# A decoder block on one core: the first norm's root on ScalarE, four orders of work, and the sums inside the last half tiles

## The reference

```python
mod  = silu(c) @ w_ada + b_ada                     # six vectors: shift1, scale1, gate1, shift2, scale2, gate2
h    = rms_norm(x, norm1_w) * (1 + scale1) + shift1
proj = h @ w_in                                    # 8 retention heads (q, k, v, gate), 8 differential heads (q, k, v)
y    = concat(retention(proj), diff_attention(proj))   # each head normed: group norm, or RMS norm
x    = x + gate1 * (y @ w_out)
h2   = rms_norm(x, norm2_w) * (1 + scale2) + shift2
x    = x + gate2 * (relu(h2 @ w_mlp1) ** 2 @ w_mlp2)   # inner width 8192
out  = rms_norm(x, final_norm_w)
```

## Time and profile before

| | us |
|---|---|
| runs, median of 3 (lowest, highest) | 2343.6 (2343.4, 2343.84) |
| the profiled execution, time | 2344.19 |
| its span, from first to last instruction | 2342.4 |
| mean granted clock of TensorE | 0.998 |
| busy: PE, DVE, ACT, POOL | 2320.1, 1256.4, 721.7, 90.7 |
| moved by DMA | 327.21 MB |

### The profile page before, as it was taken

How to read it: one execution, slowest core, us unless ns; L and a number is a source line. 1 busy time by engine, 2 the same in 40 slices (tenths; PEclk the granted TensorE clock), 3 DMA queues, 4 the chain that set the end, 5 groups by cost and what they waited for, 6 DMA issues and landing times.

```text
span 2342.4 us, 28296 instructions
## 1 busy us (share of the span) xinstructions
PE 2320.1 (99%) x10432; PEld 1891.1 (81%) x10432; DVE 1256.4 (54%) x1577; ACT 721.7 (31%) x1013; POOL 90.7 (4%) x59
## 2 busy tenths in 40 slices
PE   8999999999999999999999999999999999999998
PEld 5578888887888888888888888888888888888887
DVE  8989888866666675633333333333333333333354
ACT  3333333344445322421321321322222222222233
POOL 0011112101010000000000000000000000000000
PEclk9999999999999999999999999999999999999999
DMA  9965767622223573222222222222222222222222
GB/s 388 410 240 205 260 244 261 232 81 81 81 79 106 201 282 122 99 96 93 99 99 98 90 98 98 92 98 97 98 98 90 98 98 96 99 92 98 99 90 99
DMA packets 89575, 327.21 MB, mean 140 GB/s; under 512 B 8625, under 2 KB 9137, under 8 KB 89521
## 3 DMA queue, kind: packets, MB, share of 16 engines
q1 hardware_dynamic: 89232, 326.34, 38.8%
q10 hardware_dynamic: 290, 0.16, 0.0%
HBM read 322.27 MB, written 4.19 MB: 139 GB/s over the span
## 4 chain that ended last, share of the span: by engine, by line
PE 92%; DMA 3%; DVE 2%; issue 1%; ACT 0%; POOL 0%; ACTq 0%; POOLq 0%; DVEq 0%
PE bank L478 29%; PE bank L482 29%; PE bank L479 29%; DMA prob<-ada 3%; PE bank L689 1%; PE bank L655 1%; DVE w_lo L1209 1%; DVE ada_sb L1215 0%; PE bank L680 0%; PE bank L594 0%; PE bank L523 0%; PE bank L535 0%; PE bank L672 0%; PE bank L827 0%; PE bank L633 0%
## 5 line engine op out<-in xcount | busy, mean ns | idle before, releaser
L478 PE MATMUL bank<-act_hi,w_hi 128*128 128x512 f32 x2016 | 790.7, 392 | 0.3 <-ACT w_hi L885 0.3
L479 PE MATMUL bank<-act_lo,w_hi 128*128 128x512 f32 x2016 | 785.3, 390 | 0.0
L885 ACT ACTIVATE w_hi<-raw 128x1024 fp32r<-128x1024 f32 x393 | 415.0, 1056 | 835.4 <-PE bank L482 825.8
L1209 DVE TENSOR_TENSOR w_lo<-raw,w_hi 128x1024 fp32r<-128x1024 f32 x393 | 496.3, 1265 | 293.6 <-ACT w_hi L885 280.1
L482 PE MATMUL bank<-act_hi,w_lo 128*128 128x512 f32 x2016 | 498.2, 389 | 0.1
L478 PEld LDWEIGHTS bank<-act_hi,w_hi 128*128 128x128 f32 x2016 | 378.4, 188 | 81.2 <-ACT w_hi L885 2.3
L482 PEld LDWEIGHTS bank<-act_hi,w_lo 128*128 128x128 f32 x2016 | 378.3, 188 | 79.1 <-DVE w_lo L1209 0.5
L479 PEld LDWEIGHTS bank<-act_lo,w_hi 128*128 128x128 f32 x2016 | 378.7, 188 | 77.9
L478 PE MATMUL bank<-u_hi,w_hi 128*128 128x512 f32 (+1 forms) x1040 | 401.6, 387 | 0.0
L479 PE MATMUL bank<-u_lo,w_hi 128*128 128x512 f32 (+1 forms) x1040 | 400.2, 386 | 0.0
L1631 DVE SCALAR_TENSOR_TENSOR xy<-bank,modr,xy 128x512 f32 (+1 forms) x141 | 105.8, 750 | 412.3 <-PE bank L482 412.3
(11 more groups left out here) (176 smaller groups left out, 1304.7 us busy)
## 6 DMA issues: line engine op xcount, KB each, us to landing
raw<-weights SPq DMA_DIRECT2D x400, 512.0 KB, 3.3
ada_sb<-ada SPq DMA_DIRECT2D x78, 1024.0 KB, 5.1
xy<-x_t SPq DMA_DIRECT2D x16, 512.0 KB, 4.8
prob<-ada SPq DMA_DIRECT2D x8, 1024.0 KB, 10.4
ada<-ada SPq DMA_DIRECT2D x7, 1024.0 KB, 8.7
out<-rows_out SPq DMA_DIRECT2D x8, 512.0 KB, 4.1
ada_sb<-ada SPq DMA_DIRECT2D x4, 512.0 KB, 11.4
decay_sb<-decay SPq DMA_DIRECT2D x8, 256.0 KB, 3.3
```

The costliest lines, as they stand in the source:

```text
L478: pe.matmul(acc, stationary, hi, start=first, stop=False)
L479: pe.matmul(acc, stationary, lo, start=False, stop=False)
L885: nc.scalar.activation(w_hi[:, w], raw[:, r], ACT.Copy).then_inc(hi_ready, 1)
L1209: nc.vector.tensor_tensor(w_lo[:, w], raw[:, r], w_hi[:, w].bitcast(F32), ALU.subtract).then_inc(lo_ready, 1)
```

## The change

- *First root.* `token_mean(1)` and `token_root(1)` are gone. ScalarE loads the table of ln and exp after its last SiLU, computes exp(-0.5 ln(mean + eps)) from the bank of sums, and VectorE refines it in three 128x4 operations (`first_root`).
- *First stage.* Row 1 is loaded whole and dotted behind the root; the cast of the identity moves in between the sums of squares. For each even tile `act_lo` is now made ahead of `w_lo`, except for the last (14), whose `w_lo` goes ahead of the dot of row 30.
- *Four orders.* Head 0: `means_of_v` ahead of the modulation dot. The head before the first differential one: `var_eps` ahead of `rest_w`. Second norm: `normed_part(2, 0)` ahead of `rest_w`. First up group: `w_hi` of its ninth chunk (`C_MLP + 9`) after two of the four tiles instead of after all.
- *The end.* `last_sums(0)` and the transpose of tile 15's first half run inside `down_part(6, ...)`, before the seventh of the eight blocks of its first two passes. Half 0 is scaled as soon as its root is there, and the left half rows no longer wait for the last tile. In `last_sums` the wait for the last square stands behind the first four sums. The third row's left half is scaled and stored in two quarters, nine stores in all.
- GpSimd's roots count one mean less (`pool.wait_ge(tok_v_ready, n - 1)`).

```diff
@@ -134,7 +134,7 @@
 RESTS = (9, 11, 1, 3, 5, 7, 13)
-HALF_ROWS = (0, 1, 2 * KT - 1)
+HALF_ROWS = (0, 2 * KT - 1)
 SPLIT = tuple(k for k in range(KT) if k not in WHOLE)
@@ -181,8 +181,10 @@
     if not a.above(A_RET):
-            return a.base % NADA_1, a.base // NADA_1 + (1 if a.base % NADA_1 >= 2 else 0)
-    return a.place(NADA), a.value(NADA, -(-A_RET // NADA_1) - A_RET // NADA)
+        slot = a.base % NADA_1
+        return slot, a.base // NADA_1 + (1 if slot else 0)
+    slot = a.place(NADA)
+    return slot, a.value(NADA, A_RET // NADA_1 - A_RET // NADA + (1 if slot else 0))
@@ -232,6 +234,7 @@
         minus_half = sb("minus_half", [P128, TB])
+        ln_eps = sb("ln_eps", [P128, 1])
         mod1 = sb("mod1", [P128, KT, 2])
@@ -354,6 +357,7 @@
         newton, half_ready, turned = sem("newton"), sem("half_ready"), sem("turned")
+        first_ln, first_exp, first_newton = sem("first_ln"), sem("first_exp"), sem("first_newton")
         rotated_hi, rotated = sem("rotated_hi"), sem("rotated")
@@ -455,23 +459,33 @@
                     load_raw(Count(C_MLP + j, (4, i)))
-            for part in range(2):
-                for half in range(2):
-                    cols = slice(half * HALF, (half + 1) * HALF)
-                    for tb, scaled in ((2 * part, scaled_v), (2 * part + 1, scaled_s)):
-                        sp.wait_ge(scaled, 2 * part + half + 1)
-                        sp.dma_start(out[tb * P128:(tb + 1) * P128, cols], rows_out[:, tb, cols]).then_inc(out_written, 16)
-            sp.wait_ge(out_written, 32 * TB)
+            def store(tb, cols, scaled, count):
+                sp.wait_ge(scaled, count)
+                sp.dma_start(out[tb * P128:(tb + 1) * P128, cols], rows_out[:, tb, cols]).then_inc(out_written, 16)
+
+            left, right = slice(0, HALF), slice(HALF, D)
+            store(0, left, scaled_v, 1)
+            store(1, left, scaled_s, 1)
+            store(0, right, scaled_v, 2)
+            store(1, right, scaled_s, 2)
+            store(2, slice(0, HALF // 2), scaled_v, 3)
+            store(2, slice(HALF // 2, HALF), scaled_v, 4)
+            store(3, left, scaled_s, 3)
+            store(2, right, scaled_v, 5)
+            store(3, right, scaled_s, 4)
+            sp.wait_ge(out_written, 16 * 9)
...
         def _(pe):
-            def split_products(pairs, s, done=chunk_done):
+            def split_products(pairs, s, done=chunk_done, between=None, at=None):
...
                 for i, acc, hi, lo, first, _, ready in pairs:
+                    if at is not None and i == at:
+                        between()
                     if ready is not None:
@@ -828,11 +842,11 @@
-            def down_part(b, s, part, done):
+            def down_part(b, s, part, done, between=None, at=None):
...
                 split_products([(i, bank[b][:, cols], u_hi[:, i, cols], u_lo[:, i, cols], i == 0, i == BLOCKS - 1, None)
-                                for i in range(BLOCKS)], s, done)
+                                for i in range(BLOCKS)], s, done, between, at)
@@ -847,9 +861,10 @@
                 pe.wait_ge(ssq_ready, TAIL_SUMS + KT - 1 + part)
-                pe.wait_ge(sq_ready, TAIL_SQUARES + KT + 2 * part)
                 blocks = (2 * part, 2 * part + 1)
                 for n, source in enumerate((ssq, sq[:, 1])):
+                    if n == 1:
+                        pe.wait_ge(sq_ready, TAIL_SQUARES + KT + 2 * part)
                     for tb in blocks:
@@ -865,9 +880,11 @@
             turn_part(KT - 2, 0, KT - 1)
-            down_part(6, s0 + 30, 1, chunk_done)
-            last_sums(0)
-            turn_part(KT - 1, 0, KT)
+            def first_rows_end():
+                last_sums(0)
+                turn_part(KT - 1, 0, KT)
+
+            down_part(6, s0 + 30, 1, chunk_done, first_rows_end, 6)
             down_part(7, s0 + 31, 1, chunk_done)
@@ -985,7 +1002,7 @@
-                act.wait_ge(half_ready, 2)
+                act.wait_ge(half_ready, 3)
                 act.wait_ge(ve_ready, hp + 1)
@@ -1049,6 +1066,12 @@
                     nc.scalar.activation(silu_c[:, i * TOK:(i + 1) * TOK], bank[i][:], ACT.Silu).then_inc(silu_ready, 1)
+            load_table(LN_EXP_SET)
+            act.wait_ge(half_ready, 3)
+            act.wait_ge(mean_done, 1)
+            nc.scalar.activation(tok_r[:], ps_a[:, 0:TB], ACT.Ln, scale=LN_SCALE, bias=ln_eps[:, 0:1]).then_inc(first_ln, 1)
+            act.wait_ge(first_ln, 1)
+            nc.scalar.activation(tok_r[:], tok_r[:], ACT.Exp, scale=-0.5, bias=ln_shift[:, 0:1]).then_inc(first_exp, 1)
             act.wait_ge(vec_landed, 16)
@@ -1146,7 +1169,8 @@
                     for half in range(2):
-                        round_w(s0 + (2 * t + half + 1))
+                        if not (first and t == 0 and half == 0):
+                            round_w(s0 + (2 * t + half + 1))
                     take_u(g, 4 * q + t, t, s0 + (2 * t + 2), SPARE_UP if first and t == 0 else None)
@@ -1155,6 +1179,8 @@
             for t in range(4):
+                if t == 2:
+                    round_w(Count(C_MLP + 9))
                 take_u(0, t, t, Count(C_MLP + 8))
@@ -1179,7 +1205,8 @@
                 act.wait_ge(tok_r_ready, 4 + tb // 2)
-                act.wait_ge(tile_ready, KT + 2 * (tb // 2))
+                if half == 1:
+                    act.wait_ge(tile_ready, KT + 2 * (tb // 2))
                 row = rows_out[:, tb, half * HALF:(half + 1) * HALF]
@@ -1193,8 +1220,8 @@
             last_part(KT - 1, 0, 2)
+            scale_row(1, 0)
             last_part(KT - 2, 1, 3)
-            scale_row(1, 0)
             scale_row(1, 1)
@@ -1231,6 +1258,16 @@
                                                ALU.mult, ALU.add, to).then_inc(dot_done if half else half_dotted, 1)
+
+            def first_root():
+
+                dve.wait_ge(first_exp, 1)
+                nc.vector.scalar_tensor_tensor(tok_v[:], ps_a[:, 0:TB], NORM_EPS, tok_r[:], ALU.add, ALU.mult)\
+                    .then_inc(first_newton, 1)
+                dve.wait_ge(first_newton, 1)
+                nc.vector.scalar_tensor_tensor(tok_v[:], tok_v[:], -0.5, tok_r[:], ALU.mult, ALU.mult).then_inc(first_newton, 1)
+                dve.wait_ge(first_newton, 2)
+                nc.vector.scalar_tensor_tensor(tok_r[:], tok_v[:], 1.5, tok_r[:], ALU.add, ALU.mult).then_inc(tok_r_ready, 1)
@@ -1309,6 +1346,9 @@
                     nc.vector.tensor_tensor(ssq, ssq, square_at(m), ALU.add).then_inc(ssq_ready, 1)
+                    if m == 9:
+                        dve.wait_ge(ident_landed, 16)
+                        nc.vector.tensor_copy(ident_r[:], ident_early).then_inc(const_ready, 1)
@@ -1468,8 +1508,10 @@
                     at = j - 1 if head1 else j
-                    if at == 1:
+                    if at == 1 and not head1:
                         means_of_v(h - 1)
+                    if j == 5 and dif:
+                        var_eps(h - 1)
                     if not (head1 and j == 0):
@@ -1477,12 +1519,13 @@
                         rotate_q(h, s0 + 2, dif)
-                    if j == 5:
+                    if j == 5 and not dif:
                         var_eps(h - 1)
...
                         decay_strips(h - 1)
+                        means_of_v(h - 1)
                     for _ in range(slots[j]):
@@ -1522,25 +1565,25 @@
             first_square_sums()
-            dve.wait_ge(ident_landed, 16)
-            nc.vector.tensor_copy(ident_r[:], ident_early).then_inc(const_ready, 1)
             dve.wait_ge(vec_landed, 16)
...
             half_dot(0, 0)
-            token_mean(1)
             dve.wait_ge(silu_ready, 4)
             half_dot(0, 1)
-            half_dot(1, 0)
-            half_dot(1, 1)
+            first_root()
+            dot1(0, 1)
             normed(0, 0)
...
             for k in range(1, KT):
+                if k == KT - 1:
+                    rest_w(Count(k - 1))
                 dot1(k, 0)
...
                 if behind_split:
-                    rest_w(Count(k - 1))
                     modulated_rest(0, k - 1)
+                    if k < KT - 1:
+                        rest_w(Count(k - 1))
                     normed(0, k)
@@ -1665,9 +1708,9 @@
             modulated_rest_part(1, 0)
+            normed_part(2, 0)
             rest_w(Count(C_MLP))
             token_mean(3)
-            normed_part(2, 0)
             normed_part(3, 0)
@@ -1754,11 +1797,12 @@
-            def scale_row(tb, half):
+            def scale_row(tb, first, last):
                 dve.wait_ge(tok_r_ready, 4 + tb // 2)
-                dve.wait_ge(tile_ready, KT + 2 * (tb // 2))
-                row = rows_out[:, tb, half * HALF:(half + 1) * HALF]
+                if last > HALF:
+                    dve.wait_ge(tile_ready, KT + 2 * (tb // 2))
+                row = rows_out[:, tb, first:last]
                 nc.vector.tensor_scalar(row, row, tok_r[:, tb:tb + 1], None, ALU.mult).then_inc(scaled_v, 1)
@@ -1773,24 +1817,25 @@
```

(19 more changed lines are left out.)

## The result

The changed kernel takes 2359.1 us (median; 2358.7 to 2359.8) where the kernel before, on the same chip, takes 2343.7. The ratio is 1.0067 with the interval 1.0057 to 1.0077. The forecast was 2340.3 us, its range ended at 2342.0, and slower had been given a chance of 0.03.

The account below looks back on a forecast made before the run. PE was taken to bound most of the kernel, bytes the first stage, stores the end. Terms 0.59 + 0.32 + 0.66 + 0.42 + 0.5 + 0.8 = 3.3 us took the median 2343.6 to 2340.3 us; range 2338.7 to 2342.0.

Parts of the forecast that it names:

- the sum: Whole kernel: the gains at the stage end, four reordered waits and the output end add up to 3.3 us.
- start, inside the stage: First norm's root 0.8 us sooner and `act_lo` ahead of `w_lo`: both worth 0, covered by the stream of bytes.
- stage end: End of the first stage: chunk 14's `w_lo` ahead of row 30's dot brings later work 0.59 us sooner; bounds 0.3, 1.1.
- head 0, `means_of_v`: Head 0, before its values are used: `means_of_v` ahead of a 2.3 us dot readies `v_tok` sooner, about 0.32 us.
- `var_eps`: First differential head: `var_eps` ahead of a `w_lo` gets out of PE's way, 0.66 us.
- second norm: `normed_part(2, 0)` ahead of `w_lo` removes PE's wait for `act_hi`, 0.42 us; 0.1 comes off if `w_lo` is late.
- first up tiles: First up group: `w_hi` of chunk 9 rounded after two tiles instead of four removes PE's wait, about 0.5 us.
- tail: Output end: earlier sums and stores end the kernel 0.8 us sooner, with one break in the stream; bounds 0.4 and 1.4.
- The start counts too: Rival: the first root's 0.8 us reaches the end, giving 4.1 us, 2339.5; chance 0.17 together with all upper bounds.
- The first power is slow wherever it stands: Rival: GpSimd's 1.99 us first-run price moves to the second norm, about 0.5 us lost, 2340.8; chance 0.08.
- PE at the lower clock: Rival: shifted early PE work keeps the 1.2 GHz level longer, slower from 13 us on, near 2347; chance 0.03.
- Replaced by others: Rival: other waits 0.2 us later replace those removed, gain below 1.8 us, around 2342.5; chance 0.10.

## Why the prediction was wrong, point by point

**The failed step** is the sum, which has a term for every wait and none for PE's work. The prediction took the products' 0.23 us as given (24 of 0.23 us in a pair of chunks) and said of the gains that "PE runs without a wait behind each of them, so what is saved stays saved". It never counted the new tensor. `ln_eps` moved the moving operand of 3,024 products by 32 bytes against the weights: the kernel before with that displacement alone was 18.5 us slower. The diff names the allocation. No row of before could price its effect, since there every operand stands at distance 0, but the rows gave the scale: 92% of the chain is PE, and 1% of 0.2267 us on 3,024 products is 6.9 us, twice the whole sum.

**The rest held.** In the kernel with `ln_eps` out of the way, from the starts of the n-th product against the kernel before:

| term | forecast, us | measured, us |
|---|---|---|
| start, inside the stage | 0 | 0 (root back: no change; the new waits for `xy` too) |
| stage end | 0.59 | 0.59 (from the landing of row 30 to the start of product 400: 19.86 to 19.90, mean 19.88, in the thirteen kernels with the old order; 19.27 to 19.32, mean 19.29, in the five with the new one) |
| head 0, `means_of_v` | 0.32 | 0.40 (products 400 to 600) |
| `var_eps` | 0.66 | 0.59 (1800 to 2000) |
| second norm | 0.42 | 0.49 (4000 to 4200) |
| first up tiles | 0.50 | 0.62 (4200 to 4400) |
| tail | 0.8 | 0.83 (product 4400 to the end of the execution: 1360.23 before, 1359.40 here, 1360.22 with the old end put back); timed 0.88 |
| sum | 3.3 | 3.52; from the landing of row 30 to the end 3.50; timed 3.81 |

A wait's figure plus 0.16 us was the right price of a hand-over, within 0.12 us each time.

**The tail's hole.** In the kernel with `ln_eps` behind the heads' tensors, the first part's sums start at 2322.46, the stores at 2325.19, and the last rows' power ends at 2330.60 (compare):

```profile
2322.46 0.50 PE L869 MATMUL bank<-inv_d,ssq 128*128 128x1 f32 x4
...
2325.19 8.97 SPq L464 DMA_DIRECT2D out<-rows_out  x9
...
2329.91 0.69 POOL L1840 TENSOR_TENSOR tok_r<-tok_v,minus_half 128x2 f32<-128x2 f32 x1 [5.54 <-DVE tok_v L1798]
```

The stores start 4.7 us sooner than in the kernel before, where 3.9 had been written. The sums start 4.49 sooner, 3.05 of it from upstream (2.5 in the forecast; 0.4 is an earlier row 30) and 1.44 from their new place (1.43 in the forecast), and the power takes 0.69 us where it had taken 0.92.

The stream breaks once, as forecast, for 0.7 us where 0.5 had been worked out: the window there moved 254 GB/s in 2 us, against 399 in the one ahead (columns as in the earlier trace rows).

```profile
2328.00:2330.00 2.00, 1.44 (x12) 1.12 (x10) 0.97 (x3) 0.81 (x2) 0.09 (x1) 1.00 1.01 399
2330.00:2332.00 2.00, 0.00 (x0) 0.00 (x0) 1.26 (x4) 1.21 (x2) 0.60 (x1) 1.00 0.64 254
```

**The rivals.** *The start counts too*: refuted by the root put back. *The first power is slow wherever it stands*: refuted, the first power of the changed kernel is that of the second norm and takes 0.70 us (at 920.64), as the same one did before behind another (at 922.49), so the 1.99 went with its place or its four columns. *PE at the lower clock*: the one rival with the right sign, and not what happened: the granted clock stands at the full level from 26.56 to 2351.03 us of the changed kernel without a break (27.42 to 2334.83 before), and its first eight products with chunk 0 take 3.48 us and the next eight 2.01, as before. *Replaced by others*: true inside the first stage alone, where 2.9 us of waits for `xy` came in and cost nothing; behind it no wait took the place of those that went, and the table has the gains. The side "slower" had one mechanism only and so 0.03.

**The rest of the difference.** The displacement alone and the change without it sum to 18.5 - 3.8 = 14.7 us; 15.4 were measured. The traces say where the 0.7 lies. Row 30 lands at times between 114.52 and 115.89 us in the eighteen profiles, early and late with the old order and with the new. From its landing to the end of the profiled execution the kernel before takes 2228.64 us, the one with 32 bytes of `pad` 2247.69, the changed one 2243.97, and the changed one without the displacement 2225.14. So behind the landing the displacement costs 19.05, the change gains 3.50 without it and 3.72 with it, and the two add up to within 0.3 us. By these profiles what is left of the 0.7, and of the timed 3.81 against 3.50, lies ahead of the landing. Why a row lands a microsecond sooner in one execution than in another, no run tells.

**Left open.** What in the memory or in TensorE makes a distance cost, and why it reaches two products beyond the last displaced load.

## What to carry to other kernels

A new tensor is an edit to every tensor behind it. Where PE is the bound, compare the addresses before and after, keep each moving operand at the distance from the weights that the fast kernel has (here 0 modulo 512 bytes), and put new small tensors last or pad them to that multiple (in the run with `w_lo` moved by 32 bytes, 480 bytes behind it kept the other products at their old 227 ns). And when a change is small against the work that it leaves alone, the risk is in that work: one look at the mean duration of each unchanged group (here 390 against 395 ns) tells more than all the waits.

## What the runs showed of the hardware

TensorE's spacing at 512 columns and the full 2.4 GHz level depends on where the moving row and the weights stand to each other in a partition: 226.7 ns when they agree modulo 512 bytes, 228.6 to 236.4 otherwise, for f32 bits read as `fp32r`, each product loading its own 128 x 128 weights. What in the memory or the engine does this was not tried.

The Trainium skill, SBUF — State Buffer, SBUF: two separate sides, says that only the port shared by VectorE and GpSimd causes contention among the engines, and that PE never waits on anyone. These runs agree in that moving `raw`, `relu` and `usq`, which other engines read and write, cost nothing (2343.6 and 2343.8 us). They add that TensorE's own two operands can cost each other time: its spacing goes from 226.7 to as much as 236.4 ns with their distance.

By the Trainium skill, TensorE: Matmul & The Clock Gate, Back-to-back issue gap, a single product of 512 columns has an isolated gap of about 216 ns at the warm clock, and in a stream of loads and products the spacing is about 131 ns. The products with split weights, each behind a load of its weights, came on average no lower than 226.7 ns in any kernel here. That is 11 ns more than the page's isolated figure, at the best placement, and far from its figure for a stream; the measurement decides.
